# The seventh bunch of experts keeps out of the four buffers that the last bunch's first items and the next layers' weights go to

## The reference

```python
# 32 experts, each token goes to 2 of them
def block_ffn(args):
    xb, e = args
    return (jax.nn.silu(xb @ w_gate[e]) * (xb @ w_up[e])) @ w_down[e]
# w_gate, w_up: (32, 1024, 256); w_down: (32, 256, 1024), float32
```

## Time and profile before

| what | us |
|---|---|
| median of 3 runs | 734.92 |
| lowest, highest | 734.64, 738.69 |
| profiled execution, its device time | 740.1 |
| profiled execution, its span | 738.2 |
| TensorE busy in the span | 660.7 (89%) |
| VectorE, ScalarE busy | 352.3 (48%), 330.4 (45%) |
| mean granted TensorE clock | 0.967 |
| read from HBM | 165.96 MB |

### The profile page before, as it was taken

The page is one execution under the profiler, slowest core; times in us unless marked ns, Lnnn a source line. Parts: engine busy times, 40 slices in busy tenths (PEclk is TensorE's granted clock), DMA queues, the critical chain, the costliest instruction groups (busy, mean ns, idle before and its releaser), DMA issues.

```text
span 738.2 us, 11783 instructions
## 1 busy us (share of the span) xinstructions
PE 660.7 (89%) x4605; PEld 512.8 (69%) x4606; DVE 352.3 (48%) x817; ACT 330.4 (45%) x776; POOL 43.8 (6%) x57
## 2 busy tenths in 40 slices
PE   6989999999899999969856999998979999889986
PEld 5867998689545644616421589877859899778876
DVE  1543657646511021101000357887774577886643
ACT  3465655531111121202010253777865556888642
POOL 6001000000000000000000132010000020100000
PEclk9999999999999999989885999999989999999999
DMA  9995325896999999999769938026263080081301
GB/s 273 340 287 184 124 65 173 270 304 249 378 387 417 408 415 412 412 417 408 308 209 417 342 103 291 9 72 214 82 204 115 1 265 22 11 275 58 115 1 58
DMA packets 94681, 167.84 MB, mean 227 GB/s; under 512 B 4270, under 2 KB 75712, under 8 KB 90528
## 3 DMA queue, kind: packets, MB, share of 16 engines
q1 hardware_dynamic: 92272, 160.88, 61.1%
q0 software_dynamic: 2224, 6.10, 2.5%
q10 hardware_dynamic: 128, 0.08, 0.0%
HBM read 165.96 MB, written 1.07 MB: 226 GB/s over the span
## 4 chain that ended last, share of the span: by engine, by line
PE 60%; SPq 12%; DVE 9%; DMA 8%; ACT 8%; issue 3%; DVEq 0%; ACTq 0%
PE psum L922 10%; SPq L786 10%; PE psum L923 10%; PE psum L924 10%; PE psum L1337 5%; PE psum L1293 4%; PE psum L1352 2%; PE psum L1227 2%; DMA values<-in_w_expert_up_dram 2%; DMA mixT<-in_w_expert_up_dram 2%; PE psum L965 2%; PE psum L1057 2%; DMA ring<-in_w_in_dram 2%; PE psum L1274 2%; DVE w_low L2349 2%
## 5 line engine op out<-in xcount | busy, mean ns | idle before, releaser
L922 PE MATMUL psum<-a_high,w_high 128*128 128x256 f32 x512 | 150.8, 295 | 9.1 <-DVE w_low L2349 4.6
L923 PE MATMUL psum<-x_low,w_high 128*128 128x256 f32 x512 | 146.0, 285 | 0.0
L924 PE MATMUL psum<-a_high,w_low 128*128 128x256 f32 x512 | 145.9, 285 | 0.0
L922 PEld LDWEIGHTS psum<-a_high,w_high 128*128 128x128 f32 x512 | 99.2, 194 | 18.9 <-issue 6.8
L2349 DVE TENSOR_TENSOR w_low<-ring,w_high 128x1024 fp32r<-128x1024 f32 (+1 forms) x73 | 100.9, 1394 | 17.9 <-ACT w_high L1677 17.9
L1677 ACT ACTIVATE w_high<-ring 128x1024 fp32r<-128x1024 f32 (+1 forms) x79 | 96.1, 1220 | 13.6 <-DMA ring<-in_w_in_dram 10.3
L923 PEld LDWEIGHTS psum<-x_low,w_high 128*128 128x128 f32 x512 | 99.4, 194 | 0.1
L924 PEld LDWEIGHTS psum<-a_high,w_low 128*128 128x128 f32 x512 | 99.3, 194 | 0.0
L1337 PE MATMUL psum<-ring,q_c 128*32 128x512 f32 x336 | 64.9, 708 | 27.0 <-DMA ring<-in_w_expert_up_dram 18.3
L922 PE MATMUL psum<-w_high,a_high 128*128 128x256 f32 x240 | 69.4, 289 | 0.7 <-DVE mix_low L2360 0.7
L1337 PEld LDWEIGHTS psum<-ring,q_c 128*32 128x32 f32 x336 | 16.6, 127 | 64.6 <-issue 63.9
(11 more groups left out here) (346 smaller groups left out, 1175.6 us busy)
## 6 DMA issues: line engine op xcount, KB each, us to landing
ring<-in_w_in_dram SPq DMA_DIRECT2D x36, 1024.0 KB, 9.0
ring<-in_w_expert_down_dram SPq DMA_DIRECT2D x22, 1024.0 KB, 17.3
ring<-in_w_expert_gate_dram SPq DMA_DIRECT2D x42, 512.0 KB, 12.6
ring<-in_w_expert_up_dram SPq DMA_DIRECT2D x42, 512.0 KB, 14.3
ring<-in_w_out_dram SPq DMA_DIRECT2D x12, 1024.0 KB, 5.1
ring<-in_w_mem_kv_dram SPq DMA_DIRECT2D x4, 1024.0 KB, 15.0
k_c<-in_w_expert_down_dram SPq DMA_DIRECT2D x3, 1024.0 KB, 17.4
xT<-in_w_expert_gate_dram SPq DMA_DIRECT2D x4, 512.0 KB, 11.0
```

Of the source, the lines that this page charges most:

```text
L922: pe.matmul(dst, left[0], right[0], start=first, stop=False)
L923: pe.matmul(dst, left[0], right[1], start=False, stop=False)
L924: return pe.matmul(dst, left[1], right[0], start=False, stop=last)
```

## The change

It changes `expert_slots()` alone, that is, which buffer an item lies in. Bunches 0 to 5 are as before. Bunch 6 (the seventh) takes the buffer given away longest ago that is not one of 0, 1, 2, 3. Bunch 7 keeps its two rules, and its items 4 to 11 come out elsewhere because the row of free buffers is another. No instruction is added or removed: the same loads and matmuls in the same order, with other addresses and other waits.

```diff
     at = [k for _, k in sorted(FIRST_LOADS)]
     free = [k for k in at if k not in ONCE]
     for i in range(len(at), PER_BUNCH * BUNCHES):
-        last = i >= PER_BUNCH * (BUNCHES - 1)
-        j = i % PER_BUNCH
-        at.append(next(k for k in free if not last or (k == NEXT_LAYERS[j] if j < AT_ONCE
-                                                       else k not in NEXT_LAYERS + MORE_SLOTS)))
+        b, j = divmod(i, PER_BUNCH)
+        if b < BUNCHES - 2:
+            k = free[0]
+        elif b == BUNCHES - 2:
+            k = next(k for k in free if k not in NEXT_LAYERS)
+        elif j < AT_ONCE:
+            k = NEXT_LAYERS[j]
+        else:
+            k = next(k for k in free if k not in NEXT_LAYERS + MORE_SLOTS)
+        at.append(k)
         free.remove(at[-1])
         free.append(at[-1])
     return at
```

## The result

| | median us | lowest, highest | runs |
|---|---|---|---|
| before | 736.37 | 734.18, 741.28 | 6 |
| after | 726.19 | 723.84, 727.69 | 6 |

The ratio of after to before is 0.9852, 95% interval 0.9813 to 0.9891: about 10.9 us faster. That is the direction that was forecast, and less of it: 726.19 lies above the range that ended at 724.5, and the ratio's whole interval lies above 0.9807, which is what a gain of 14.2 us gives. The profiled execution of after has a span of 721.9 us, 16.3 less than that of before. So the two profiles show more than the forecast and the timed runs less. Of all executions of the kernel before, four at 744.5 to 746.2 us, over 1.5% above its fastest, are left out of the comparisons.

A forecast was written before the change was run, and what follows sets the result against it. The prediction took loads to bound the experts' stretch, with a hole made by SP's 27.2 us wait before bunch 7. Removing it lets bunch 7's second half begin 14.2 us earlier: 734.92 - 14.2 = 720.7 us, 8-in-10 range 718.0 to 724.5.

The forecast's parts named there:

- What bounds the kernel, and the dip: Loads bound the experts' stretch; SP's 27.2 us wait before bunch 7's first load makes the DMA dip at 364 to 376.
- The new waits are covered: New waits in bunches 6 and 7's loads cost 0, hidden by a load backlog of 15.91 us from issue to landing.
- The stop of 2.3 us: At item 9 of bunch 6, SP waits about 2.3 us for `y_ready` of bunch 5; cost taken as 0, at most 2.3.
- The stream of 30.4 us a bunch: Loads bring one bunch per 30.4 us, 414 GB/s, so bunch 7's second half can begin at 386.59.
- The slower stream: Rival: from 364 on, 385 GB/s gives 722.9 (0.13, shared with a hole); 349 GB/s gives 726.3 (0.05).
- ... and the first half runs 379.6 to 383.2 at full clock: Bunch 7's first half follows bunch 6's add-back directly; TensorE then idles 3.4 us until the second half at 386.6.
- a spacing over 31: Sign of being wrong: second halves of successive bunches more than 31 us apart, where 30.4 was expected.
- less than a microsecond: TensorE's clock during the 3.4 us idle before bunch 7's second half moves the rest by less than this.
- The missing 14.2 us are the dip: Bunch 7's second half begins 44.65 us behind bunch 6's instead of about 30.4; the change recovers the 14.2.
- The layers behind: From `add_back` of bunch 7 on nothing is tied to an absolute time, so the 14.2 us reach the end whole.
- The rival in which the clock falls because TensorE idles less: Slower than before, in the layers after 438: each per cent of clock costs up to 3 us; chance 0.02.
- The base: The starting median, 734.92 us, from which 14.2 was subtracted, with a microsecond and a half of noise each way.

The follow-up runs named there:

- after_gate_y: The changed kernel with bunch 7's first load waiting for bunch 6's down matmuls (`y_ready`), as before the change: 737.0 us, ratio 0.9975 to before.
- after again: The changed kernel run again unchanged, for a second profile and interval: 725.6 us (median of 4), ratio 0.986 to before.
- after_no_branch: The changed kernel without the overflow branch on TensorE behind bunch 6: 726.1 us (median of 4), ratio 0.9862 to before.
- the kernel with the layers held: The kernel before with a few extra matmuls where TensorE waits in the two layers behind the experts: 735.7 us (10 runs, mean 736.1).
- after_gate_gu: The changed kernel with bunch 7's first load waiting for bunch 6's second half (`gu_ready`): 727.8 us (median of 4), ratio 0.9835 to before.

## Why the prediction was right or wrong

**What bounds the kernel, and the dip: right.** One wait of SP made the hole, and with that wait put back (after_gate_y) the hole and the time come back.

**The new waits are covered: right.** The four down loads of bunch 6 were issued in 6.33 us from 341.80, as before in 6.35, with no wait in between. The stop of 2.3 us that I had expected at item 9 was too long: I had divided 6.35 by four, but the first of the four issues takes 2.96 us, so SP comes to item 9 at 344.8, behind `y_ready` of bunch 5 at 344.4. In after again it does wait, 0.9 us, and the DMA has no hole (waits of SP's queue, 338 to 348):

```profile
SPq L795 <- PE psum L1358: 0.9, 1, 0.9
```

A wait of 13 us put in on purpose made no hole either.

**The stream of 30.4 us a bunch: right.** after_no_branch, in which no other thing stands before it, begins bunch 7's second half at 386.81, 30.35 behind that of bunch 6. The slower stream, the rival that made the upper part of my range, did not come (406 GB/s). By the Trainium skill ("DMA: Bandwidth & Descriptors", section "Where 436 GB/s comes from"), with its 358 GB/s, the prediction had an estimated 725.4. That is close to the 726.19 measured, but by luck and not by that road: the trace of after has 411 GB/s from 200 to 364 us and 406 from 364 to 376.

**"... and the first half runs 379.6 to 383.2 at full clock": wrong.** The add-back did end at 379.58, but the first half began at 384.37 and the second at 389.50, 32.1 behind that of bunch 6, where I had named a spacing over 31 as a sign of being wrong. I looked at what the wait of 10.99 us was for and not at what else lay under it. TensorE reads a flag and branches between bunches 6 and 7, 4.8 us, and this is laid bare when the wait goes. I had worked out that cost for SP's queue (0.9 us) and not for TensorE's. In that profile it costs nothing only because the last down item lands at 398.5 anyway: down begins at 398.6, where I had 397 to 398. With the clock low (after again) it stands in the chain, and "less than a microsecond" for the clock in the new timeline was too little too: 117.2 against 115.8.

**"The missing 14.2 us are the dip", and so "I take 14.2": the term of the sum that was mis-sized.** It measured 10.9 us by the ratio of the runs (10.2 between the medians, 11.4 between the means of 92 and of 10 executions). It is right for the execution it was read from: the stretches are 130.2 and 115.7 to 117.2, 13 to 14.5 apart. It is not a constant of the kernel. The loads of bunch 7 were released by the end of bunch 6, which contains a half whose length hangs on the clock: 6.4 us in my profile, 3.6 with the clock held. With the clock held the release comes 2.4 us earlier (16.1 against 18.5), the stretch is 127.2 or 126.5, and the change has that much less to give: 11. That executions of both kinds occur is shown by the mean clocks; that the usual execution is of the short one is shown for the kernel with the layers held (8 of 10) and stays inferred for the kernel before as it is, from its mean gain of 11.4. I did work out what the clock does to the *new* timeline (less than a microsecond) and never asked what it does to the old one, from which the gain is subtracted. My profile, at a clock of 0.967 and 740.1 us, was of the long kind. That this stood 5.2 us over the median of the runs shown, which I took for an offset of the profile, was the hint: part of the difference can lie in the very stage that is being priced.

**The layers behind.** "From `add_back` of bunch 7 on nothing is tied to an absolute time, so the gain reaches the end whole" holds on the mean: with the clock held there, the distance of the two kernels is 11.6 to 11.7, as in the timed runs. It doesn't hold for one execution against one other: the two first profiles differ by 16.3, of which 13.3 was there at 415.76 against 429.07, and 3 came from the clock in the layers. The rival in which the clock falls because TensorE idles less did not come; the mean clock rose from 0.972 to 0.977.

**The base.** I took 14.2 off a median of 3 runs, 734.92. In six runs the median is 736.37, in 92 the mean is 737.3. Between the medians, of the 5.5 us by which the forecast was too low, 1.5 are the base and the other 4 the gain. My range gave the base a microsecond and a half of noise; three runs out of a spread of 733 to 742 deserved more.

## What to carry to other kernels

A gain is a difference of two timelines, so both must be priced in their other states: look at what the start of a hole hangs on, and if a part of it has two lengths (here a half of a bunch at either clock), the hole has two sizes. When a long wait is about to go, list everything on that engine that runs under it without being seen (flags, branches, code), not only what the wait is for. And a wait in a queue of loads can be free while it is shorter than the time from issue to landing of what was issued before it: here 13.0 us cost nothing against 15.9, and 26.6 cost the whole gain. Nothing between the two was run.

## What the runs showed of the hardware

A flag read and a branch over a body of code that isn't run took TensorE 4.79 us (384.37 - 379.58; 4.76 to 4.88 in the other profiles of the changed kernel), against 0.9 us on SP's queue for its own in the profile of before. With the branch taken out of TensorE's code the idle time is gone.

The same kernel runs from 733 to 742 us on one core, and the mean granted clock, 0.981 to 0.961, goes with it: over these 92 executions a hundredth of it is some 4 us. Where TensorE waits 1 to 2 us in otherwise full work, the lower clock appears in some executions and not in others: behind the wait of 2.0 us near 492 us it came in after again and after_gate_gu, and not in after, which has the same wait. With a few matmuls at such places the runs spread less: 723.0 to 726.3 (9) against 722.7 to 728.6 (10).
